# Round 3 of a two-block transformer kernel in seven products, with the attention parts around it at other steps

## The reference

```
h = rmsnorm(x, norm_attn[l])
proj = h @ w_in[l]
qa, ka, va, qb, kb, vb = jnp.split(proj, splits, axis=-1)
...
s = jnp.einsum('bhcqe,bhcke->bhcqk', qblk, kt, preferred_element_type=jnp.float32) * (d ** -0.5)
p = jax.nn.softmax(s, axis=-1)
a = p[:, :, 0] - lam * p[:, :, 1]
return jnp.einsum('bhqk,bhke->bhqe', a, vt.astype(jnp.float32))
...
yb = (rmsnorm(yb, subln[l], SUBLN_EPS) * (1.0 - lam_init)).astype(x.dtype).reshape(B, S, B_WIDTH)
x = x + jnp.concatenate([ya, yb], axis=-1) @ w_out[l]
```

## Time and profile before

| | |
|---|---|
| median of 3 executions | 2471.29 us (2470.95 to 2472.79) |
| the profiled execution's own time | 2470.19 us |
| its span, first to last instruction | 2468.2 us |
| PE busy | 2454.1 us, 99% |
| DVE busy | 2158.7 us, 87% |
| ACT busy | 1594.3 us, 65% |
| mean granted TensorE clock | 0.999 |

### The profile page before, as it was taken

One profiled execution on the slowest core, in us unless ns is written; L12 is line 12 of the kernel. 1 busy time (PEld: TensorE's weight loads), 2 busy tenths in 40 slices (PEclk: granted clock), 3 DMA queues, 4 the chain that ended last, 5 costly groups with the idle time before them and its releaser, 6 DMA issues.

```text
span 2468.2 us, 28393 instructions
## 1 busy us (share of the span) xinstructions
PE 2454.1 (99%) x11207; PEld 2028.8 (82%) x11207; DVE 2158.7 (87%) x1704; ACT 1594.3 (65%) x1518; POOL 54.6 (2%) x56
## 2 busy tenths in 40 slices
PE   9999999999999999999999999999999999999998
PEld 7888888788888888788888888888888888888887
DVE  6977677999999999979788787877799999999997
ACT  7655556677777777775565565544666666776666
POOL 0000000000000000000000000000000000000000
PEclk9999999999999999999999999999999999999999
DMA  9546445555555555565355456546467777777775
GB/s 324 187 137 231 145 147 195 182 209 210 208 211 205 211 208 208 194 222 196 137 201 187 165 197 225 185 171 239 171 200 235 234 224 236 229 231 229 230 247 160
DMA packets 251875, 503.58 MB, mean 204 GB/s; under 512 B 8608, under 2 KB 8608, under 8 KB 251488
## 3 DMA queue, kind: packets, MB, share of 16 engines
q1 hardware_dynamic: 238976, 474.56, 55.0%
q0 software_dynamic: 11904, 25.64, 5.6%
q10 hardware_dynamic: 864, 1.57, 0.2%
HBM read 478.67 MB, written 2.10 MB: 195 GB/s over the span
## 4 chain that ended last, share of the span: by engine, by line
PE 71%; DVE 23%; issue 4%; ACT 1%; DMA 0%; DVEq 0%; SPq 0%; ACTq 0%
PE acc L901 18%; PE acc L905 18%; PE acc L903 17%; DVE w_lo L2055 16%; PE misc L901 4%; PE misc L905 4%; PE misc L903 4%; DVE w_raw L2021 1%; DVE w_raw L2027 1%; PE misc L946 1%; DVE w_raw L2023 1%; PE misc L954 1%; DVE w_raw_more L2027 1%; PE acc L918 1%; PE acc L914 1%
## 5 line engine op out<-in xcount | busy, mean ns | idle before, releaser
L2055 DVE TENSOR_TENSOR w_lo<-w_raw,w_hi 128x2048 fp32r<-128x2048 f32 x462 | 1045.7, 2274 | 122.6 <-ACT w_hi L1474 122.4
L1474 ACT ACTIVATE w_hi<-w_raw 128x2048 fp32r<-128x2048 f32 x462 | 879.0, 1907 | 372.7 <-PE acc L905 188.8
L901 PE MATMUL acc<-w_hi,xt_hi 128*128 128x512 f32 x1132 | 448.0, 396 | 0.2
L905 PE MATMUL acc<-w_hi,xt_lo 128*128 128x512 f32 x1132 | 441.4, 390 | 0.0
L903 PE MATMUL acc<-w_lo,xt_hi 128*128 128x512 f32 x1132 | 440.7, 389 | 0.0
L905 PEld LDWEIGHTS acc<-w_hi,xt_lo 128*128 128x128 f32 x1132 | 212.4, 188 | 45.0
L901 PEld LDWEIGHTS acc<-w_hi,xt_hi 128*128 128x128 f32 x1132 | 212.6, 188 | 44.4 <-issue 1.8
L903 PEld LDWEIGHTS acc<-w_lo,xt_hi 128*128 128x128 f32 x1132 | 212.7, 188 | 42.6
L1474 ACT ACTIVATE w_hi<-w_raw_more 128x2048 fp32r<-128x2048 f32 (+1 forms) x95 | 178.6, 1883 | 71.4 <-DVE w_raw_more L2027 16.0
L2055 DVE TENSOR_TENSOR w_lo<-w_raw_more,w_hi 128x2048 fp32r<-128x2048 f32 (+1 forms) x95 | 212.4, 2239 | 2.5 <-ACT w_hi L1474 2.5
L901 PE MATMUL misc<-w_hi,xt_hi 128*128 128x512 f32 x412 | 162.2, 394 | 1.4 <-DVE w_lo L2055 1.4
(11 more groups left out here) (424 smaller groups left out, 4315.1 us busy)
## 6 DMA issues: line engine op xcount, KB each, us to landing
w_raw<-in_w_in SPq DMA_DIRECT2D x132, 1024.0 KB, 5.0
w_raw<-in_w_ffn_up SPq DMA_DIRECT2D x61, 1024.0 KB, 6.8
w_raw<-in_w_ffn_down SPq DMA_DIRECT2D x42, 1024.0 KB, 6.0
w_raw<-in_w_out SPq DMA_DIRECT2D x32, 1024.0 KB, 5.1
w_raw<-in_w_gate SPq DMA_DIRECT2D x30, 1024.0 KB, 6.4
w_raw_more<-in_w_ffn_up SPq DMA_DIRECT2D x27, 1024.0 KB, 7.8
w_raw<-in_w_down SPq DMA_DIRECT2D x25, 1024.0 KB, 7.5
w_raw<-in_w_up SPq DMA_DIRECT2D x24, 1024.0 KB, 6.5
```

Of the source, the lines that this page charges most:

```text
L901: nc.tensor.matmul(bank, hi[:, j, :], w_hi[:, t % RING, j, :], start=first and j == 0, stop=False, skip_group_check=shared)
L905: end = nc.tensor.matmul(bank, lo[:, j, :], w_hi[:, t % RING, j, :], start=False, stop=last and j == C - 1, skip_group_check=shared)
L1474: nc.scalar.activation(w_hi[:, t % RING, rows], raw_tile(steps[t].slot)[:, rows], ACT.Copy).then_inc(hi_ready, 1)
L2055: nc.vector.tensor_tensor(w_lo[:, t % RING, rows], raw_tile(steps[t].slot)[:, rows], w_hi[:, t % RING, rows].bitcast(F32), ALU.subtract).t ...
```

## The change

Round 3 joins `UNIT_ROUNDS`, so its eight steps for queries and keys become eleven, of which seven are half steps. The parts of round 2, which stood one per step at round 3's q0 to v0, now stand at G3, P2, P4, v0, v1, v2 and v3 (parts 0 to 6), and part 8 at D0 of down 1. The parts of round 3, which stood at v2, v3 and the four steps of down 1 and first of down 2, now start one step later: part 0 at v3 (together with part 6 of round 2), parts 1 to 6 at the next six steps; part 8 stays at D2 of down 2. The eight steps of queries and keys of round 3 held eight loads of weights, and the eleven hold eight as well.

```
-UNIT_ROUNDS = (1, 2, 4, 5, 6, 7)
+UNIT_ROUNDS = (1, 2, 3, 4, 5, 6, 7)
...
-             2: early(3, 9),
-             3: [ROUND_T[3] + 10 + k for k in range(9)],
+             2: [STEP[("round", 3), name] for name in ("G3", "P2", "P4", "v0", "v1", "v2", "v3")],
+             3: [STEP[("round", 3), "v3"]] + [DOWN_T[1] + k for k in range(6)],
...
-    return {(r, t): s for r, ts in steps.items() for s, t in enumerate(ts)}
+    parts = {(r, t): s for r, ts in steps.items() for s, t in enumerate(ts)}
+    parts[2, DOWN_T[1]] = parts[3, DOWN_T[1] + 6] = 8
+    return parts
```

## The result

| | before | changed kernel |
|---|---|---|
| median | 2471.54 us (2470.95 to 2472.91, 11 executions) | 2476.12 us (2474.92 to 2479.16, 11 executions) |
| profiled execution | 2470.19 us, span 2468.2 | 2479.16 us, span 2477.2 |
| PE busy | 2454.1 us | 2455.2 us |
| mean granted TensorE clock | 0.999 | 0.997 |

The ratio is 1.0022, with a 95% interval of 1.0014 to 1.0030: 4.6 us longer in the medians, clear of no difference, from a change that takes twelve matmuls away. The interval reaches under the prediction's line of 0.2%. The profiled execution is the slowest of the eleven, 3.0 us over the median.

What follows compares the result with a forecast made beforehand. PE, busy 99% of the span, was taken to bound the kernel, each new wait adding one for one. Waits of 7.6 us less 2.7 for matmuls gave +4.8 on 2471.3: 2476.1 us, range 2469.5 to 2481.0.

Steps and rivals of the forecast that it cites:

- The twelve matmuls, −2.7: Round 3's queries and keys: 180 matmuls instead of 192, at 0.227 us each, saving 2.7 us.
- No wait in the seven products: Round 3's seven products: DVE finishes its extra work with 2 us to spare, so PE waits 0 there.
- rival 2: P7 to P4 of round 3: DVE is late for the seven products, net +8 to +10, about 2480 us; chance 0.12.
- P2, 0.9: Half step P2: scores of head 1 wait 0.9 us for the exponentials to free their banks.
- P4, 0.9: Half step P4: transposes wait 0.9 us for the probabilities of head 0.
- The turn at v0, 3.3: Turn of round 3's queries at v0 waits 3.3 us for banks just filled by head 3's scores; bounds 0 and 7.7.
- D0, 0.8: Start of down 1: scores of round 3's head 1 wait 0.8 us, exponentials standing behind round 2's norm.
- D1, 1.7: Next step of down 1: transposes wait 1.7 us for head 0's probabilities, behind splits and `yt_lo`.
- Sum of the waits, 7.6: The five PE waits, 0.9 + 0.9 + 3.3 + 0.8 + 1.7, total 7.6 us; 5.5 to 9.7 with roundings.
- Part 6 of round 3 is now one step ahead of part 8: End of round 3's attention: the norm needs 5.6 us, values plus a full step give 6.3, so no wait.
- Rival 3: Clock falls at the turn's wait, v1 runs at half rate, 5.4 us more, 2481.5 us; chance 0.06.
- Rival 1: The waits hide and only the matmuls count: 2468.6 us, up to 2472 with two waits left; chance 0.17.

Runs made afterwards that it cites:

- steps_alone: Changed kernel with round 3 keeping its eight full steps, so only the parts are moved; 2479.93 us, ratio 1.0037 to the kernel before.
- bank3_mid: Changed kernel with round 3's sum in bank 3 and round 2's parts at U2, U3, P7, G3, v0, v1, v2; 2470.25 us, ratio 1.0000 to before.
- rope_k_v0: Changed kernel with the rope of round 3's keys moved from P4 to v0, behind the maximum of head 3; 2475.58 us, ratio 1.0022 to before.
- order_reversed: Changed kernel with round 3's parts ahead of round 2's at v3 and D0 on all engines; 2475.53 us, ratio 1.0022 to before.
- again: The changed kernel, unedited, measured and profiled once more; 2477.47 us, ratio 1.0028 to the kernel before.
- bank3_full_steps: Changed kernel with round 3's sum in bank 3 and round 2's parts beginning on full steps G2, U2, U3, G3; 2470.28 us, ratio 0.9997 to before.
- before_r3_late: The kernel before, with only round 3's parts one step later (part 8 unmoved); 2470.88 us, ratio 1.0002 to before.
- bank3_spread: bank3_full_steps with round 3's keys turned at v1 and its parts back where the kernel before had them; 2470.20 us, ratio 0.9999 to before.

## Why the prediction was right, and where it was wrong

The forecast was 2476.1 us, the median 2476.12. The hundredths are luck. The forecast difference was 4.8 us, and the three comparisons of this kernel gave 4.6, 7.1 and 6.1. Their ratios, 1.0022, 1.0028 and 1.0027, all lie over the line of 0.2%, with intervals that reach a little under it. "Slower" and "same" at 0.48 and 0.49 were even odds, and a difference that stands so near the line leaves them so; what held is the account of where the time goes.

- **The twelve matmuls, −2.7.** Right: 11,195 for 11,207 instructions, at 0.227 us each. The half steps P2 and P4 take 2.86 and not 2.72 (281.18 to 284.04), since their first matmul comes more slowly behind the scores.
- **No wait in the seven products.** Right, and with it rival 2 falls: PE is full over 35.4 us there, and no row has it waiting for `w_lo` in round 3. DVE's and the loads' extra work is hidden.
- **P2, 0.9, and P4, 0.9.** Both waits came, on the lines named, at 0.72 and 0.55. Their cause, a chain of 3.45 us that doesn't fit beside a half step, is borne out by steps_alone, where they are gone, and by bank3_mid, where one comes back behind a half step. The forecast counted from start to start; so counted they cost 0.79 and 0.71, which is 0.1 and 0.2 under it. The forecast added a restart of 0.3 to 0.4 to such waits; at the turn, where the timeline shows it, PE's row stands 0.15 behind the end of the last exponential (302.35 + 0.21, then 302.71).
- **The turn at v0, 3.3.** It was 3.14 in the row and 3.3 from start to start: the largest term, and right in size. Three parts of its working were off and made up for each other: the queue of DVE behind the scores was put at 0.35 us (17.8 against 17.45) and was 0.7, the restart at 0.35 and was 0.15, the values beside it at 0.9 and were 1.2 in the row (298.41 + 1.16). The maximum itself was well placed, 17.9 us behind the scores of head 0 (281.18 to 299.11) for 17.8. The bounds were not: with the sum's own terms the chain alone leaves 17.45 + 3.45 + 0.35 − 18.4 = 2.9 us, so the lower bound of 0 couldn't be met by any queue, and the text's "which follows the queue" names the smaller part. rope_k_v0, which took 1.33 out of the queue and won 0.5, shows it.
- **D0, 0.8, and D1, 1.7.** They were 0.59 and 1.38 in the rows and 0.75 and 1.54 from start to start, at the lines named, and order_reversed moved them as their mechanism asks. (The prediction's last paragraph has the scores' line wait in three places; its own sum has two, P2 and D0, and two came.)
- **Sum of the waits, 7.6.** The five sum to 6.38 in the rows and to 7.1 from start to start. The steps of the prediction that failed are not in any of them but in what it left out, twice:
  - *The end of round 3's attention.* "Part 6 of round 3 is now one step ahead of part 8 ... Nothing." PE indeed waits for nothing there. But DVE leaves the downs 0.9 us later against PE (0.82 to 0.89 all the way from 375 to 447 us of before's time, in again, bank3_full_steps and before_r3_late), and PE meets that at the first feed-forward, 100 us on, where the gap grew from 0.35 to 1.21. before_r3_late has it without the rest of the change, bank3_spread loses it by moving the parts back. I asked what is late at the next step and not at the next place where PE already waited for DVE.
  - *The clock.* Rival 3, at 0.06 and 5.4 us. It happened, in the profile of the changed kernel itself: half level from 301.55 to 308.38, at a cost of 2.7 us and not 5.4. As forecast and rival they were put too exclusively: the clock doesn't fall instead of the forecast's waits but on top of them, in part of the executions. Of five profiles with a wait of 3.1 us and more, three show it. The row of the program's end bore on it, at 2.6 us of idleness; "PE works up to the wait and right after it" was no reason against it. The Trainium skill's warning on idle gaps between bursts of matmuls (TensorE: Matmul & The Clock Gate, Why this matters for your kernels) is borne out here by these three profiles, and not by the other two.

So the terms came to 4.8 − 0.5 (waits too large) + 0.9 (the feed-forward) = 5.2, which is what the two profiles without half level show, and a half level in part of the executions comes on top. The mean of the three comparisons is 5.9. That the first of them gave 4.6 and so met the forecast is luck; it lies under the traces.

Rival 1, that the waits hide, falls with the first profile. Its condition can be met: with the sum in bank 3 and the parts on full steps (bank3_full_steps) no attention line waits. Its price is not met even so: the kernel is as fast as before, not 2.7 us faster. No version measured was faster than before by more than the comparisons can tell; the lowest are 0.9997 (bank3_full_steps) and 2470.2 us (bank3_spread). Of the 2.7 us of matmuls, the rows for small waits take 1.5 back in either; their traces are only 0.55 and 0.28 us under before, and the 0.6 to 0.9 us between is not followed up.

## What to carry to other kernels

A step that is made shorter is also less cover. Before halving steps beside a dependent chain, compare the chain (here 3.45 us from maximum to last exponential) with the new step (2.72), and look at whatever shares its buffers: the turn behind the scores cost more than the twelve matmuls gave, and moving it one step on gave 3.3 us back in the traces, 4.9 in the medians measured beside it. When an engine with slack is made late, look for the next place where the busy engine already waited for it, however far on.

## What the runs showed of the hardware that was not expected

- A single wait of PE between full bursts can be followed by the lower clock level: 6.8 us of it at waits of 3.14 and 3.17 us, beginning 2.0 and 2.4 us into the wait, and 3.4 us after one of 3.66. The same 3.15 and 3.17 us in two more profiles of the same kernel were followed by full clock, and so was one of 2.67. Near the start of the program, where PE goes from twenty small matmuls to its first products, 3.4 us of the lower level followed waits of 1.86, 2.04, 2.25 and 2.38 us in four profiles; waits of 1.26 to 1.78 us in the other nine were followed by full clock.
- The 6.8 us of half level cost 2.7 us, not 3.4, since part of it (1.2 us, to 302.71) lay in the wait itself, and the stretch behind has small transposes too.
